# Second attention of a two-layer encoder: the halves of an output formed one step after its sum, the query weights split two heads ahead

## What is computed

```
q = (c_q @ w_uq)    -> per head 64 plain + 32 rotary columns
kv = (c_kv @ w_ukv) -> per head 64 key + 64 value columns
s = (q_nope . k_nope + rope(q_rope) . k_rope) * 96 ** -0.5
p = softmax(where(chunk(key) <= chunk(query), s, -inf))
o = p @ v
...
x = LN(alpha * x + (1 + g1) * (concat(o) @ w_o))
```

## Time and profile before

| what | value |
|---|---|
| median of 3 runs | 3033.82 us (3033.09 to 3034.83) |
| profiled execution | 3037.47 us, its span 3035.8 us |
| TensorE matmul busy | 2708.2 us (89%) |
| VectorE busy | 1680.8 us (55%) |
| ScalarE busy | 1189.8 us (39%) |
| GpSimd busy | 327.6 us (11%) |
| mean granted TensorE clock | 0.95 |

### The profile page before, as it was taken

How to read it: one execution, slowest core, us unless ns; L and a number is a source line. 1 busy time by engine, 2 the same in 40 slices (tenths; PEclk the granted TensorE clock), 3 DMA queues, 4 the chain that set the end, 5 groups by cost and what they waited for, 6 DMA issues and landing times.

```text
span 3035.8 us, 37829 instructions
## 1 busy us (share of the span) xinstructions
PE 2708.2 (89%) x12716; PEld 2229.4 (73%) x12716; DVE 1680.8 (55%) x2862; ACT 1189.8 (39%) x2125; POOL 327.6 (11%) x346
## 2 busy tenths in 40 slices
PE   3888888877999999999997888888699999999996
PEld 2666666666778888888775777777577888888884
DVE  4566666664765344444575777777467333232346
ACT  3355555553451221203364566656326212130223
POOL 0000000000111000015043222222001000000000
PEclk8988899987999999999998999999899999999997
DMA  8122222225234233241232111111442211111122
GB/s 307 56 70 66 67 70 69 70 99 185 84 107 136 75 104 104 70 120 46 83 111 66 30 29 26 33 26 35 163 129 84 72 46 49 48 48 48 48 83 77
DMA packets 328831, 245.78 MB, mean 81 GB/s; under 512 B 40679, under 2 KB 303126, under 8 KB 327710
## 3 DMA queue, kind: packets, MB, share of 16 engines
q1 hardware_dynamic: 312910, 185.82, 20.8%
q0 software_dynamic: 14736, 50.34, 5.5%
q10 hardware_dynamic: 1088, 8.39, 0.7%
HBM read 215.12 MB, written 33.59 MB: 82 GB/s over the span
## 4 chain that ended last, share of the span: by engine, by line
PE 64%; DVE 13%; ACT 10%; issue 9%; DMA 3%; ACTq 0%; DVEq 0%; SPq 0%; POOL 0%
PE PA L1665 32%; PE SC L1665 25%; PE VB L1751 3%; DVE H L1198 2%; DVE soft L1580 2%; ACT H L734 2%; ACT X L750 1%; DVE W L1107 1%; ACT X L1033 1%; ACT W L685 1%; PE TB L1672 1%; DMA x_rows<-in_x 1%; DVE H L1237 1%; ACT H L728 1%; DVE X L1602 1%
## 5 line engine op out<-in xcount | busy, mean ns | idle before, releaser
L1665 PE MATMUL PA<-U,W 128*128 128x512 f32 x3840 | 955.8, 403 | 80.8 <-DVE W L1107 46.3
L1665 PEld LDWEIGHTS PA<-U,W 128*128 128x128 f32 x3840 | 731.0, 193 | 251.6 <-issue 56.1
L685 ACT ACTIVATE W<-raw 128x1024 fp32r<-128x1024 f32 (+2 forms) x262 | 260.2, 994 | 818.2 <-PE PA L1665 390.0
L1665 PE MATMUL SC<-U,W 128*128 128x512 f32 x2064 | 484.1, 393 | 3.8 <-DVE W L1107 3.6
L1665 PEld LDWEIGHTS SC<-U,W 128*128 128x128 f32 x2064 | 389.4, 189 | 90.9 <-DVE W L1107 5.1
L1107 DVE TENSOR_TENSOR W<-raw,W 128x1024 fp32r<-128x1024 f32 (+2 forms) x262 | 314.5, 1201 | 103.7 <-ACT W L685 102.2
L1665 PE MATMUL PA<-H,W 128*128 128x512 f32 x1536 | 358.7, 392 | 3.2 <-DVE W L1107 3.2
L1665 PE MATMUL SC<-H,W 128*128 128x512 f32 x1536 | 354.4, 390 | 0.0
L1665 PEld LDWEIGHTS PA<-H,W 128*128 128x128 f32 x1536 | 288.5, 189 | 64.5 <-DVE W L1107 3.6
L1665 PEld LDWEIGHTS SC<-H,W 128*128 128x128 f32 x1536 | 288.4, 188 | 60.7 <-issue 1.0
L734 ACT ACTIVATE H<-TB 128x512 fp32r<-128x512 f32 (+3 forms) x216 | 108.0, 500 | 217.4 <-PE TB L1672 216.0
(11 more groups left out here) (214 smaller groups left out, 3064.2 us busy)
## 6 DMA issues: line engine op xcount, KB each, us to landing
raw<-in_ffn_w SPq DMA_DIRECT2D x160, 512.0 KB, 4.0
ada<-in_ada_w POOLq DMA_DIRECT2D x80, 512.0 KB, 4.7
U<-attention_out SPq DMA_DIRECT2D x4, 3584.0 KB, 17.4
raw<-in_da_w_qkv SPq DMA_DIRECT2D x24, 512.0 KB, 4.8
ada_first<-in_ada_w ACTq DMA_DIRECT2D x4, 2048.0 KB, 18.4
attention_out<-ostage SPq DMA_DIRECT2D x32, 256.0 KB, 2.8
raw<-in_da_w_o SPq DMA_DIRECT2D x16, 512.0 KB, 4.1
X<-residual SPq DMA_DIRECT2D x4, 2048.0 KB, 11.3
```

Source lines behind the costliest of these rows:

```text
L685: nc.scalar.activation(W[:, slot, 0, 0:kt * P], raw[:, slot, 0:kt * P], ACT.Copy).then_inc(w_hi, 1)
L1665: ins = mm(bank, W[:, slot, a, kt * P:(kt + 1) * P], moving(b, kt)[:, cols], start=kt == first and (a, b) == SPLIT[0], stop=kt == last and ...
```

## The change

- VectorE's `out_lo` no longer follows in `sum_out`. `out_hi` and `out_lo` of a pair stand one step later: in steps 4 and 6 for pairs 0 and 1, in steps 0 and 2 of the next head for pairs 2 and 3, ahead of the weight splits.
- The query weights of head h + 2 are split at the end of step 6 of head h, where those of head h + 1 had been split at the end of step 0 of head h; the first head still does its neighbour's in step 0.
- The key and value weights of head h + 1 are split in step 0 of head h, not in step 2.
- `values1` waits for each group of four transposed blocks when it comes to it, not for the last group at the start.

```diff
@@ ScalarE, heads1
+                    if s in (0, 2) and not is_first(h):
+                        out_hi(a1, h - 1, 2 + s // 2, VD, osum[0:VD, :])
+                    if s in (4, 6):
+                        out_hi(a1, h, s // 2 - 2, VD, osum[0:VD, :])
                     if s == 1 and not is_first(h):
                         out_bottom(h - 1, 3)
-                        out_hi(a1, h - 1, 3, VD, osum[0:VD, :])
                     if s in (3, 5, 7):
                         out_bottom(h, (s - 3) // 2)
-                        out_hi(a1, h, (s - 3) // 2, VD, osum[0:VD, :])
+                    if is_first(h) and s == 0:
+                        split_uq(g0, 2 * i, h + 1, a1["pj_ready"], 4 * h + 3)
                     if proj and s == 0:
-                        split_uq(g0, 2 * i, h + 1, a1["pj_ready"], 4 * h + 3)
-                    if proj and s == 2:
                         split_hi(g0 + 1, 2 * i, KVT, a1["pj_ready"], 4 * h + 4)
+                    if not last and s == 6:
+                        split_uq(g0 + 2, 2 * i, h + 2, a1["pj_ready"], 4 * h + 7)
...
+            out_hi(a1, HEADS1 - 1, 2, VD, osum[0:VD, :])
             out_bottom(HEADS1 - 1, 3)
             out_hi(a1, HEADS1 - 1, 3, VD, osum[0:VD, :])
@@ VectorE, sum_out
                     .then_inc(a1["o_fin"], 1)
-                out_lo(a1, h, pair, VD, osum[0:VD, :])
@@ VectorE, heads1
+                    if s in (0, 2) and not is_first(h):
+                        out_lo(a1, h - 1, 2 + s // 2, VD, osum[0:VD, :])
+                    if s in (4, 6):
+                        out_lo(a1, h, s // 2 - 2, VD, osum[0:VD, :])
                     if s == 1 and not is_first(h):
                         sum_out(h - 1, 3)
                     if s in (3, 5, 7):
                         sum_out(h, (s - 3) // 2)
+                    if is_first(h) and s == 0:
+                        split_lo(g0, 2 * i, QT)
                     if proj and s == 0:
-                        split_lo(g0, 2 * i, QT)
-                    if proj and s == 2:
                         split_lo(g0 + 1, 2 * i, KVT)
+                    if not last and s == 6:
+                        split_lo(g0 + 2, 2 * i, QT)
...
+            out_lo(a1, HEADS1 - 1, 2, VD, osum[0:VD, :])
             sum_out(HEADS1 - 1, 3)
+            out_lo(a1, HEADS1 - 1, 3, VD, osum[0:VD, :])
@@ TensorE, values1
-                pe.wait_ge(a1["t_evac"], 13 * h + group_of(last, 1 if last >= 4 else 0) + 1)
                 for j in range(last + 1):
+                    if j % 4 == 0:
+                        pe.wait_ge(a1["t_evac"], 13 * h + group_of(last, j // 4) + 1)
```

## The result

The changed kernel took 3051.61 us (median of 8 runs, 3038.26 to 3059.85), the kernel before 3034.46 (8 runs, 3024.74 to 3043.96). The ratio is 1.0050, with a 95% interval of 1.0028 to 1.0071: slower by 9 to 22 us. The forecast was 3032 with a range up to 3046, so the time lies outside it, on the side that had a chance of 0.26.

A forecast was written before the change was run, and what follows sets the result against it. No engine is full; waits passed between engines bound a head, ScalarE's before `out_hi` the suspect. 14 heads times 0.31 (+4.3), -1.1, -1.4, -3.6 make -1.8: 3035.7 for the profiled execution, 3032 us as median, range 3015 to 3046.

The forecast's parts named there:

- the side that had a chance of 0.26: Whole kernel: a time slower than 3039.9 us, chance 0.26.
- Steps 2 to 6, the gain of 2.53: Steps 2 to 6 of a head: halves one step later start the low half of block 6 2.53 us earlier.
- Step 6, 2.83 added: End of step 6: `out_lo` and the query split beside GpSimd's rotation start VectorE's step 7 4.16 after L1571, not 1.33.
- taken strictly: Step 6, rival: VectorE and GpSimd exclude each other fully; split ends 4.63 after L1571, 3037.5 in all; chance 0.1.
- From there to the last pair's values is 2.57 and from these to the next head 6.77; nothing in it moves: From VectorE's step 7 to the next head: both durations stay as before, so a head is 0.31 us longer.
- The first head: Head 0, step 2: no pair 3 before it, so it loses the split's 1.15 there; 1.1 us less.
- Head 14: Head 14, step 6: no query split there, so its values come at 23.41 instead of 24.79; 1.4 us less.
- The last head: Head 15: output load starts 9.0 after head 14's last values, then 9.5 of work in place of 13.5; -3.6 us.
- The finer waits of `values1`: TensorE's values: waiting group by group brings nothing and costs nothing, since the sum of the pair before comes later.
- The rivals: Split without GpSimd's turn, 3017 (0.17); split behind rotation, 3052 (0.2); strict exclusion, 3037.5 (0.1); change without effect, 3034 (0.03).
- The slower one: End of step 6 on VectorE: the split falls behind the whole rotation, 1.42 us a head, 3052 in all; chance 0.2.
- its clause on unseen waits: Part of the 3052 us rival, chance 0.2: an unseen wait that loses the upstream gain ends alike.

The follow-up runs named there:

- e5: The changed kernel with eight unread matmuls at the end of step 7 and four ahead of the last pair's values; ratio 1.0002 to the kernel before.
- e9: The kernel of e2 with the single wait of `values1` as before, for the last transposed group; ratio 0.9911 to the kernel before, 3003.21 us.
- e2: The changed kernel with the query split put back at the end of step 0, for head h + 1; ratio 0.9899 to the kernel before.
- e3: The kernel before with only the query split moved, to the end of step 6 of the head before; ratio 1.0115.
- e4: The change without its split moves: halves one step later and finer waits, query split in step 0, key split in step 2; ratio 1.0105 to the kernel before.
- e8: The kernel before with only the key split moved, from step 2 to step 0; ratio 0.9962.

## Why the prediction was wrong

By its own steps:

- **Steps 2 to 6, the gain of 2.53: right.** In the changed trace the two rotations of a head start 15.1 apart (1765.38 and 1780.46), where the sum had 15.30 between the two L1571 and the trace of before 17.58. So 2.50 was gained here and not 2.28 (the 2.53 less the 0.25 gained ahead of the first L1571); the difference is `out_lo` in step 2, priced at 1.22 and 0.99 in the trace, at 1765.94.
- **Step 6, 2.83 added: right in kind, a little low.** 4.45 after L1576, not 4.16, so 3.12 added. The turns of the earlier trace rows hold. I had priced `out_lo` like the key split with nothing behind it; with the split behind it, it took 1.51. The page "SBUF — State Buffer" of the Trainium skill, section "Who interferes with whom", had the direction right; taken strictly it gave 4.55 (4.63 less the overlap), and the trace lies between the two, 0.10 under the rule and 0.29 over my forecast.
- **"From there to the last pair's values is 2.57 and from these to the next head 6.77; nothing in it moves": this step failed.** 2.57 held (1750.69 to 1753.26). The 6.77 became 8.27 where the clock fell (from 1753.26 to TensorE's transposes of step 2 at 1761.53) and stayed 6.77 where it did not (1786.80 to 1793.57). I moved durations from the trace of before into a head whose TensorE pauses differently, and took for granted that they come at the same clock. The trace of before could have warned me: the head of the earlier trace rows has a granted clock of 1.00, but most of its neighbours have 0.95, with a fall in step 3. A head without a fall takes 32.0 and the sum said 31.87: the wait chain was right, the duration of TensorE's own work was not. From the first mark to the fourteenth, 13 heads, it is 412.35 us before, 416.40 in e5, without falls, and 427.67 in the changed kernel: 4.05 longer without falls, where 13 times 0.31 is 4.0. Two heads in three at 1.5 more make 14 us over 14 heads.
- **The first head: 0.7 too much taken off.** From TensorE's transposes of step 2 of head 0 to the first mark it is 24.25 us where it was 24.32, so 0.07 less, and 0.31 less 1.1 promised 0.8 less. Head 0 is about 1.0 shorter than the other heads of the changed kernel in this stretch (24.25 against 25.27), as forecast; but in the kernel before it was already shorter by 0.47 (24.32 against 24.79), which the sum left out.
- **Head 14: right but for the clock.** Forecast 1.4 less; from mark to mark it is 31.27 against 31.39, since it begins with a fall (its values at 2115.53 take 3.63). In e5, without the fall, it is 29.74, 1.65 less.
- **The last head: right.** The load starts 8.94 after the last values of head 14 (2146.80), forecast 9.0; from the landing, at the start of the last L774 that waits for it (2178.18), to the end of the last half (2187.53) it is 9.35, forecast 9.5.
- **The finer waits of `values1`: right**, by e9.
- **The rivals.** None had the mechanism. The slower one named a split behind the whole rotation; the trace shows that the split goes between the second and third operations. Its time, 3052, came true for another reason, and its clause on unseen waits covers no fall of the clock. With the clock left out, the range was too low: a fall in every head would have asked for 20 us more. Together the parts give the 11.4 us of the two traces: -0.1 for the first head, +15.3 for 13 heads, -0.1 for head 14, -3.75 for the last (34.42 from mark to mark against 38.17; forecast -3.6).

The expectation of the change as a whole hides a cancellation that e2, e3, e4 and e8 take apart. The ping-pong of `out_hi` and `out_lo` that it removes and the key split together are worth 1.9 a head (e2, 31.72 to 29.81); the query split in step 6 takes 2.2 back by the wait and 0.9 by the clock. Halves without the key split's move lose too (e4): both then stand in step 2 beside the rotation, and the clock falls there in every head.

## What to carry to other kernels

Before moving an operation of VectorE that reads two SBUF operands, look at what GpSimd does in that place, and move it ahead of the operation that sets GpSimd off rather than behind it: the same two operations cost 3.3 us behind and 1.1 ahead. When a sum over a wait chain lengthens TensorE's pauses, give the matmuls behind the pause a price at the lower clock as well, as a rival of its own. Look at the granted clock of several heads, not of one: a fall can be there already and cost next to nothing until it moves onto the path. A trace with two lengths of one loop body is read by one instruction group at a fixed place, not by means.

## What the runs showed of the hardware

- Matmuls that nothing reads can pay: twelve of them a head (3.1 us of TensorE) brought the changed kernel from 1.0050 to 1.0002. Six of them, which left 0.77 and 0.93 us of pause, brought nothing that can be measured.
- What a fall of the clock costs depends on what stands behind it: 0.2 us a head in step 3 of the kernel before, where waits follow, 1.5 us in step 0 of the changed one, where none follow.
- The falls come in patterns: in step 3 in 8 of 13 heads before, in step 0 in two heads of three in the changed trace, in e3 in step 0 of every second head and step 3 of every head, in e4 in step 3 of every head. What sets the pattern was not tried.
- Two operations of VectorE behind one another beside GpSimd's rotation slow GpSimd as well: in step 6 the rotation's first operation went from 1.26 to 1.79 us, its third from 1.27 to 1.60.
- Executions of one kernel spread over 20 us (3024 to 3044 before), and the unchanged stretch ahead of the heads differed by 11.8 us between two traces. With a spread like that the two profiled executions, 3037.47 and 3038.26, hid a loss of 15 us.
